# RMS norms of two layers and the last norm: token sums on partitions, short roots and inverses, spread by TensorE

## What is computed

```python
def rmsnorm(x, g):
    x32 = x.astype(jnp.float32)
    var = jnp.mean(x32 * x32, axis=-1, keepdims=True)
    return (x32 * lax.rsqrt(var + NORM_EPS) * g.astype(jnp.float32)).astype(x.dtype)
...
    x = x + rmsnorm(mix, norm_post[l])            # end of the first block
...
    h = rmsnorm_2(x, norm_g[l]) * (1.0 + scale[:, None]) + shift[:, None]     # start of each layer
    hc = rmsnorm_2(xc, norm_g[l]) * (1.0 + scale_c) + shift_c
...
    return rmsnorm_2(x, final_norm_g)             # the end
```

## Time and profile before

| what | value |
|---|---|
| runs | 2992.14, 2998.05, 2998.65 us (median 2998.05) |
| profiled execution | 2996.14 us, span 2994.3 us |
| PE, PEld busy | 2827.3 us (94%), 2227.6 us (74%) |
| DVE, ACT, POOL busy | 1518.5 us (51%), 988.2 us (33%), 506.1 us (17%) |
| granted clock of TensorE, mean | 0.976 of 2.4 GHz |

### The profile page before, as it was taken

How to read it: one execution, slowest core, us unless ns; L and a number is a source line. 1 busy time by engine, 2 the same in 40 slices (tenths; PEclk the granted TensorE clock), 3 DMA queues, 4 the chain that set the end, 5 groups by cost and what they waited for, 6 DMA issues and landing times. The chain is left out here.

```text
span 2994.3 us, 36239 instructions
## 1 busy us (share of the span) xinstructions
PE 2827.3 (94%) x14018; PEld 2227.6 (74%) x14018; DVE 1518.5 (51%) x2060; ACT 988.2 (33%) x1709; POOL 506.1 (17%) x607
## 2 busy tenths in 40 slices
PE   7899999998769999999999999999989999989997
PEld 5666666667447868888888877788878877867785
DVE  6687877877563552125533346423253375546334
ACT  4444444444352333112212126411142232226321
POOL 2444445434331031000000002100010000002000
PEclk9999999999789999999999999999999999999998
DMA  5577777765213252223323432322313444441421
GB/s 186 188 303 302 295 303 285 303 242 183 102 57 120 91 183 70 91 100 137 120 104 121 142 149 75 116 78 94 121 50 108 141 172 144 146 175 60 162 99 56
DMA packets 111687, 447.20 MB, mean 149 GB/s; under 512 B 11440, under 2 KB 19760, under 8 KB 76208
## 3 DMA queue, kind: packets, MB, share of 16 engines
q1 hardware_dynamic: 111536, 445.16, 40.9%
HBM read 375.25 MB, written 69.86 MB: 149 GB/s over the span
## 5 line engine op out<-in xcount | busy, mean ns | idle before, releaser
L2758 PE MATMUL ps<-h_hi,w_hi 128*128 128x512 f32 x1600 | 576.9, 361 | 0.0
L2759 PE MATMUL ps<-h_lo,w_hi 128*128 128x512 f32 x1600 | 565.1, 353 | 0.0
L2760 PE MATMUL ps<-h_hi,w_lo 128*128 128x512 f32 x1600 | 561.4, 351 | 0.0
L393 PE MATMUL ps<-h_hi,w_hi 128*128 128x512 f32 (+1 forms) x1152 | 412.6, 358 | 19.8 <-DVE w_lo L352 10.3
L394 PE MATMUL ps<-h_lo,w_hi 128*128 128x512 f32 (+1 forms) x1152 | 411.9, 358 | 0.0
L395 PE MATMUL ps<-h_hi,w_lo 128*128 128x512 f32 (+1 forms) x1152 | 410.1, 356 | 0.0
L2758 PEld LDWEIGHTS ps<-h_hi,w_hi 128*128 128x128 f32 x1600 | 301.9, 189 | 49.6 <-issue 6.2
L2759 PEld LDWEIGHTS ps<-h_lo,w_hi 128*128 128x128 f32 x1600 | 301.7, 189 | 46.6 <-issue 6.2
L2760 PEld LDWEIGHTS ps<-h_hi,w_lo 128*128 128x128 f32 x1600 | 300.8, 188 | 43.8
L2534 DVE TENSOR_TENSOR w_lo<-raw,w_hi 128x2048 fp32r<-128x2048 f32 x64 | 146.4, 2288 | 311.7 <-ACT w_hi L2434 311.7
L393 PEld LDWEIGHTS ps<-h_hi,w_hi 128*128 128x128 f32 x1152 | 219.6, 191 | 55.3 <-DVE w_lo L352 12.2
(11 more groups left out here) (391 smaller groups left out, 4741.8 us busy)
## 6 DMA issues: line engine op xcount, KB each, us to landing
raw<-w_in SPq DMA_DIRECT2D x112, 1024.0 KB, 5.1
raw<-ada_w SPq DMA_DIRECT2D x96, 1024.0 KB, 8.3
raw<-w_out SPq DMA_DIRECT2D x48, 1024.0 KB, 4.9
proj<-xw SPq DMA_DIRECT2D x60, 384.0 KB, 2.6
xw<-proj SPq DMA_DIRECT2D x72, 256.0 KB, 3.3
xw<-proj SPq DMA_DIRECT2D x46, 384.0 KB, 3.4
xw<-resid SPq DMA_DIRECT2D x8, 1536.0 KB, 12.7
proj<-wide SPq DMA_DIRECT2D x32, 256.0 KB, 10.7
```

Source lines behind the costliest of these rows:

```text
L393: pe.matmul(a_[q], wh, h_hi[:, h0 + k, lo:hi], start=k == 0, stop=False)
L2758: pe.matmul(a_[q], wh, h_hi[:, k, a:b], start=k == 0, stop=False)
L2759: pe.matmul(a_[q], wh, h_lo[:, k, a:b], start=False, stop=False)
L2760: ins = pe.matmul(a_[q], wl, h_hi[:, k, a:b], start=False, stop=k == KC - 1)
```

## The change

In all four norms named above, the operands of the summing matmul change places. The squares are now the stationary operand, 128 tokens at a time, and one column of `ones` is the moving one. The result is a 128x1 column per 128 tokens, with tokens on partitions: four columns for 512 tokens, six with the context. Root and inverse are taken of 128x4 or 128x6 in `stat`. Then PE spreads the inverse back over partitions: for each 128 tokens a matmul whose stationary operand is the inverse column repeated 128 times (stride 0) and whose moving operand is the identity. ACT takes the root ahead of converting weight tile 1. PE waits for the inverse ahead of `context(0, k)` and, the second time, ahead of the last eight `context(1, k)`. Layer 1 has one root and one inverse for tokens and context together. `final_norm` reads the factor from PSUM.

```diff
+                    act.wait_ge(sum_ready.h, sum_ready.at(1))
+                    act.activation(roots[:, 0:tokens], bank(4)[:, 0:tokens], ACT.Sqrt, bias=lam[:, 7:8], scale=1.0 / D
+                                   ).then_inc(rms_ready.h, 1)
                     act.wait_ge(raw_full[1].h, raw_full[1].at(16))
                     act.activation(w_hi[:, 1, :], raw[:, 1, :], ACT.Copy).then_inc(hi_done.h, 1)
-                    act.wait_ge(sum_ready.h, sum_ready.at(1))
-                    act.activation(rms, bank(4), ACT.Sqrt, bias=lam[:, 7:8], scale=1.0 / D).then_inc(rms_ready.h, 1)
-                    if l:
-                        act.wait_ge(sum_ready.h, sum_ready.at(2))
-                        act.activation(rms_c, sums_c, ACT.Sqrt, bias=lam[:, 7:8], scale=1.0 / D).then_inc(rms_ready.h, 1)
...
-                        act.activation(rms, sum_ps, ACT.Sqrt, bias=lam[:, 7:8], scale=1.0 / D).then_inc(rms_ready.h, 1)
+                        act.activation(roots[:, 0:TB], sum_ps[:, 0:TB], ACT.Sqrt, bias=lam[:, 7:8], scale=1.0 / D
+                                       ).then_inc(rms_ready.h, 1)
...
-                    dve.reciprocal(bank(5), rms).then_inc(st.step(), 1)
-                    dve.wait_ge(st.sem, st.now)
+                    dve.reciprocal(invs[:, 0:tokens], roots[:, 0:tokens]).then_inc(inv_ready.h, 1)
+                    dve.wait_ge(spread.h, spread.at(1))
...
-                        dve.reciprocal(inv, rms).then_inc(st.step(), 1)
-                        dve.wait_ge(st.sem, st.now)
+                        dve.reciprocal(invs[:, 0:TB], roots[:, 0:TB]).then_inc(inv_ready.h, 1)
+                        dve.wait_ge(spread.h, spread.at(2))
...
                     if l:
-                        dve.wait_ge(rms_ready.h, rms_ready.at(2))
-                        dve.reciprocal(inv_c, rms_c).then_inc(st.step(), 1)
-                        dve.wait_ge(st.sem, st.now)
+                        dve.wait_ge(spread.h, spread.at(2))
...
-                    def sum_of(dst, a, b):
-                        pe.matmul(dst, ones[:], acc_sq[:, a:b], start=True, stop=False)
-                        pe.matmul(dst, ones[:], tmp[:, a:b], start=False, stop=True).then_inc(sum_ready.h, 1)
-                    sum_of(bank(4), 0, T)
+                    def spread_to(dst, q0, n, z):
+
+                        pe.wait_ge(inv_ready.h, inv_ready.at(z))
+                        for q in range(n):
+                            ins = pe.matmul(dst[:, q * P:(q + 1) * P], invs[:, q0 + q:q0 + q + 1].to_broadcast([P, P]), ident[:],
+                                            start=True, stop=True)
+                        ins.then_inc(spread.h, 1)
+                    for q in range(tokens):
+                        pe.matmul(bank(4)[:, q:q + 1], acc_sq[:, q * P:(q + 1) * P], ones[:, 0:1], start=True, stop=False)
+                        ins = pe.matmul(bank(4)[:, q:q + 1], tmp[:, q * P:(q + 1) * P], ones[:, 0:1], start=False, stop=True)
+                    ins.then_inc(sum_ready.h, 1)
+                    spread_to(bank(5), 0, TB, 1)
                     if l:
-                        sum_of(sums_c, T, W)
+                        spread_to(inv_c, TB, CT // P, 1)
                     else:
                         for k in range(KC):
                             context(0, k)
                         for k in range(KC):
                             pe.wait_ge(sq_ready.h, sq_ready.at(k + 1))
-                            pe.matmul(sum_ps, ones[:], sq_buf[k % 3], start=k == 0, stop=k == KC - 1).then_inc(sq_summed.h, 1)
+
+                            for q in range(TB):
+                                ins = pe.matmul(sum_ps[:, q:q + 1], sq_buf[k % 3][:, q * P:(q + 1) * P], ones[:, 0:1],
+                                                start=k == 0 and q == 0, stop=k == KC - 1 and q == TB - 1)
+                            ins.then_inc(sq_summed.h, 1)
                             if k >= KC // 2:
                                 context(1, k - KC // 2)
+                        spread_to(inv, 0, TB, 2)
                         for k in range(KC // 2, KC):
                             context(1, k)
...
         def final_norm():
+            roots, invs, factor = stat[:, 0:TB], stat[:, 8:8 + TB], bank(1)
...
-                    dve.reciprocal(rstd[:, 0:T], tmp[:, 0:T]).then_inc(st.step(), 1)
-                    dve.wait_ge(st.sem, st.now)
+                    dve.reciprocal(invs, roots).then_inc(inv_ready.h, 1)
+                    dve.wait_ge(spread.h, spread.at(1))
                     for k in range(KC):
                         x = xk[:, k, 0:T]
-                        dve.scalar_tensor_tensor(x, x, col("final", k), rstd[:, 0:T], ALU.mult, ALU.mult).then_inc(m1.h, 1)
+                        dve.scalar_tensor_tensor(x, factor, col("final", k), x, ALU.mult, ALU.mult).then_inc(m1.h, 1)
```

More of the change, by code:

```diff
@@ L203, in program @@
             "mask_in", "roped", "norms", "factors", "o_scaled", "turned_back", "d_done", "gate_mult"))
-        first_hi = count("first_hi")
+        first_hi, inv_ready, spread = count("first_hi"), count("inv_ready"), count("spread")
         gate_in = [count(f"gate_in{i}") for i in range(4)]
@@ L2186, in projections @@
             sq_buf = [wide[:, 0:T], wide[:, 1024:1024 + T], wide[:, 1536:1536 + T]]
-            rms = wide[:, W:W + T] if l else wide[:, T:2 * T]
-            rms_c = wide[:, W + T:2 * W]
             sum_ps, inv = (bank(4), bank(5)) if l else (bank(6), bank(7))
-            sums_c, inv_c = bank(6)[:, 0:CT], bank(7)[:, 0:CT]
+            inv_c = bank(7)[:, 0:CT]
+            tokens = W // P if l else TB
+            roots, invs = stat[:, 0:6], stat[:, 8:14]
             def scale_at(k):
@@ L2389, in read_out @@
                         ins.then_inc(gate_tanh.h if gate else staged.h, 1)
+                    act.wait_ge(sum_ready.h, sum_ready.at(1))
+                    act.activation(roots[:, 0:tokens], bank(4)[:, 0:tokens], ACT.Sqrt, bias=lam[:, 7:8], scale=1.0 / D
+                                   ).then_inc(rms_ready.h, 1)
                     act.wait_ge(raw_full[1].h, raw_full[1].at(16))
                     act.activation(w_hi[:, 1, :], raw[:, 1, :], ACT.Copy).then_inc(hi_done.h, 1)
-                    act.wait_ge(sum_ready.h, sum_ready.at(1))
-                    act.activation(rms, bank(4), ACT.Sqrt, bias=lam[:, 7:8], scale=1.0 / D).then_inc(rms_ready.h, 1)
-                    if l:
-                        act.wait_ge(sum_ready.h, sum_ready.at(2))
-                        act.activation(rms_c, sums_c, ACT.Sqrt, bias=lam[:, 7:8], scale=1.0 / D).then_inc(rms_ready.h, 1)
-                    else:
+                    if l == 0:
                         for k in range(KC):
@@ L2825, in projections @@
             on_pool = sum(low_on_pool(k) for k in range(KC))
-            for s, v in ((sum_ready, 1 + l), (rms_ready, 2), (scaled, KC), (hi_ready, KC), (shifted, on_pool), (low_ready, on_pool),
+            for s, v in ((sum_ready, 1), (rms_ready, 2 - l), (inv_ready, 2 - l), (spread, 2), (scaled, KC), (hi_ready, KC), (shifted, on_pool), (low_ready, on_pool),
                          (low_ready_v, KC - on_pool), (half_used, 1), (half_hi, 1), (half_lo, 1)):
@@ L2845, in _ @@
                 def _(pe):
-                    pe.matmul(bank(0), ones[:], acc_sq[:, 0:T], start=True, stop=False)
-                    pe.matmul(bank(0), ones[:], tmp[:, 0:T], start=False, stop=True).then_inc(m3.h, 1)
+                    for q in range(TB):
+                        pe.matmul(bank(0)[:, q:q + 1], acc_sq[:, q * P:(q + 1) * P], ones[:, 0:1], start=True, stop=False)
+                        ins = pe.matmul(bank(0)[:, q:q + 1], tmp[:, q * P:(q + 1) * P], ones[:, 0:1], start=False, stop=True)
+                    ins.then_inc(m3.h, 1)
+                    pe.wait_ge(inv_ready.h, inv_ready.at(1))
+                    for q in range(TB):
+                        ins = pe.matmul(factor[:, q * P:(q + 1) * P], invs[:, q:q + 1].to_broadcast([P, P]), ident[:], start=True, stop=True)
+                    ins.then_inc(spread.h, 1)
                 @block.scalar
@@ L2851, in _ @@
                     act.wait_ge(m3.h, m3.at(1))
-                    act.activation(tmp[:, 0:T], bank(0), ACT.Sqrt, bias=lam[:, 7:8], scale=1.0 / D).then_inc(m4.h, 1)
+                    act.activation(roots, bank(0)[:, 0:TB], ACT.Sqrt, bias=lam[:, 7:8], scale=1.0 / D).then_inc(m4.h, 1)
                 @block.vector
```

## The result

The changed kernel takes 3008.13 us (median of 5 runs, 3004.97 to 3012.73), the kernel before 2998.05 us (median of 5, 2992.14 to 3000.84). The ratio is 1.0033, 95% interval 1.002 to 1.0047: slower by 10 us, and by 6 us at the interval's near end. The profiled execution took 3004.97 us, its span 3003.2 us.

What follows compares the result with a forecast made beforehand. PE bounds the kernel (busy 2827.3 of 2994.3 us), so only its waits at the norms count. Layer 0 +10.7, layer 1 -1.0 and final norm -1.3 sum to +8.4, giving 3005 us, range 3001 to 3009.

Steps and rivals of the forecast that it cites:

- The largest term: Layer 0's second norm: the clock falls during the one-column square sums, making F +10.7 us.
- one term: Layer 1's scaling start and PE restart: forecast as -1.0 us, bounds -3.2 and +1.5.
- The clock in layer 0: Second norm's square sums: clock falls about 4 us in, steps 1.68 then 2.33 us, F +10.7.
- F: Start of DVE's scaling in a layer, taken to carry PE's restart (product behind `latent`), about 26.9 us later, one for one.
- Rival A: Layer 0's square sums: dense weight loads keep the clock up; total -3.6 us, 2992.5 us; chance 0.30.
- Layer 0's other terms: First norm: `w_lo` subtraction 2.3 us later, additions 1.8 later; second norm -2.4, so F -0.6 at 2.4 GHz.
- Short passes: Norm chains: root 0.26 us, inverse 0.17; matmul halves 0.11 us at 2.4 GHz, 0.21 at 1.2 GHz.
- rival B: Narrow sums: passes cost half, 0.055 us, with the clock high; total -7.2 us, 2989 us; chance 0.07.
- The spread: Norm chains: 8 halves returning the inverse across partitions add 1.1 us at 2.4 GHz; layer 1's 1.85 at 1.2 GHz.
- Layer 1: the term that was mis-sized: Layer 1's norm: 24 halves in 3.9 us, spread 1.85; F -1.0 us, bounds -3.2 and +1.5.
- The last norm: Final norm: -2.4 us at 2.4 GHz, -1.3 with part at 1.2 GHz; bounds -2.4 and 0.
- Rival C: Spreads: stride-0 weights or a wait cost more than the inverse replaced; 1 us more each gives 2995.5; chance 0.05.

## Why the prediction was right, point by point

The forecast was 3005 us with a range of 3001 to 3009, the median is 3008.13; the sum was +8.4, and the medians differ by 10.1. The largest term was right in mechanism and size; one term was wrong in sign, and that the total still fits is in part luck.

- **The clock in layer 0.** Right in mechanism and nearly in size. Put: it falls about 4 us into the sums, steps of 1.68 and then 2.33, F +10.7. Measured: the clock fell 2.4 us into them (1096.07 to 1098.44), behind two steps instead of some three, steps 1.70 to 1.71 and 2.34 to 2.35, F +11.61. Rows of the kernel before could not show that one-column sums do this: ahead of the fall at 124 us PE had also been idle, and the prediction drew the thin streaming from it as the cause. The run with 128 columns is what shows it. Rival A (it holds) is out; the run with 128 columns shows what it would have given, -0.6 at F as rival A put it.
- **Layer 0's other terms.** Put: POOL's subtraction 2.3 us later and the additions 1.8. Measured 2.1 (6.42 against 4.29 behind L395) and 1.64. The context's tile 0 was put at an end of 1094; it gave way to the sums at 1096.07, since the clock was low ahead of it too (0.55 from 1088.4 to 1092), and so set the start of the sums. That cost little here, but it is why the run with layer 0's order gained 1.3 and not 2.2 us. Put: F +1.8 behind them with a wide second norm, as the run with the wide form gave (1.68).
- **Short passes.** Root 0.26 and inverse 0.18 (0.19 for 6 columns), as put, to 0.02. Halves 0.11 at 2.4 GHz and 0.21 at 1.2 GHz, as put; rival B is out. They are 0.11 also with 64 and 128 moved columns, which is what the Trainium skill ("TensorE: Matmul & The Clock Gate", LDWEIGHTS) makes one expect of a load that goes by its own columns; at 1.2 GHz the trace has twice the Trainium skill's figure.
- **The spread.** Put: 1.1 us. So it is at 2.4 GHz (1.16). But in the changed kernel every spread ran at least partly at the low clock (1.73 to 2.0 for 8 halves, 2.93 for layer 1's 12), also behind the first norm of layer 0, where I had not looked for it; it cost nothing there, because POOL was later still.
- **Layer 1: the term that was mis-sized.** Put -1.0 with bounds of -3.2 and +1.5, measured +2.34, outside them. Two steps failed. First, the 24 halves were put at 3.9 us, half at each clock; all 24 ran at 1.2 GHz, 5.1 us, which is 1.2 of the 1.6 us between the -1.3 that I had and the +0.28 measured (the rest is a spread of 2.1 instead of 1.85 and the hand-overs). Second, I took it that the scaling's start carries PE's restart one for one, because both layers had 26.9 us between them; with POOL's 4.53 us subtraction moved beside DVE's first low part, that part took 3.02 us and 2.06 us were added behind F. The price was to be had beforehand, from the Trainium skill's rule named above and POOL's 4.50 us row: a low part that starts beside it ends about when it does (0.55 us later here). I had named POOL's lateness and dropped 0.3 us for it, but looked only at what POOL does late, not at what it does to DVE beside it.
- **The last norm.** Put -1.3, measured -1.78 in this profile, and between 0.0 and -2.0 in the other profiles with one-column sums. The forecast fits, but it is a draw from a range, not a figure. Its terms make -1.2 and not -1.3, too.
- **Rival C** is out: the spread costs no more than its halves.

The forecast's three terms missed by +0.9, +3.3 and -0.5 us, 3.8 together, so by the places the change costs 12.2 us. The medians differ by 10.1 and the profiled spans by 8.9: stages that the change doesn't touch gave 2 to 3 us back, and with them the total came out inside the range, 0.9 us from its end. That is luck and not part of the working.

## What to carry to other kernels

Before a wide reduction is made thin, ask what it does to TensorE's clock: here 28 us of gapless work on one-column matmuls, with some of the context's among them, ran at 1.2 GHz, and moving 128 columns where one would do cost nothing behind the weight load and gave 12 us back. An operation that is moved into the shadow of another engine's work is to be priced for both sides, as it may slow the neighbour down (0.75 to 3.02 us here). And a gain on a chain of short steps that begins with TensorE idle for some 2 us is not one number: its size depends on where the clock falls (the same last norm gained 0.0 to 2.0 us), so read several profiles.

## What the runs showed of the hardware

- In layer 0's square sums the granted clock did not follow how busy PE's rows are. With the same count and order of weight loads, one moved column per load gave 0.50 with PE busy for 11.80 of 11.80 us, and 128 gave 1.00 with 13.47 of 13.90. How many are needed between these was not tried.
- A float32 half cost 0.11 us from start to start at 2.4 GHz with 1, 64 or 128 moved columns, and 0.21 at 1.2 GHz with any of them.
- DVE's `scalar_tensor_tensor` on 128x512 took 3.02 us beside POOL's `tensor_tensor` on 128x2048, and 0.75 without it, with the same operands. POOL's next low part took 1.73 us instead of 1.28. DVE's scalings beside the same subtraction, with one input in PSUM, kept their time (1.41 for two).
